# Softmax weights turned by VectorE in 32x32 blocks and by DMA, in place of TensorE transposes

## The reference, cut to what matters

```python
q, k, v, f, z = jnp.split(h @ w_in, SPLIT0, axis=-1)      # 12 query heads, 4 key/value heads, head width 128
q, k = apply_rope(q, ...), apply_rope(k, ...)
# blocks of 128 queries; each sees its own block, the one before and the one after, and 256 context tokens
s_win = einsum('bqkgd,bjkd->bkgqj', qn, kw) * scale
s_ctx = einsum('bqkgd,bjkd->bkgqj', qn, k_ctx) * scale
logits = concatenate([sink_logits, s_ctx, s_win], -1)
p = softmax(logits, -1)                                    # the sink takes part in the sum only
out = p_ctx @ v_ctx + p_win @ vw
y = concatenate([out, fourier_mix(f, w_f)], -1)
x = x + gate * ((y * silu(z)) @ w_out)
```

## Time and profile before

| | us |
|---|---|
| median of 3 runs | 1417.44 (1417.28 to 1417.67) |
| profiled execution, span from first to last instruction | 1416.2 |
| PE busy in it | 1389.8 (98%) |
| DVE busy | 861.2 (61%) |
| ACT busy | 515.2 (36%) |
| POOL busy | 74.6 (5%) |

### The profile page before, as it was taken

One profiled execution on the slowest core, in us unless ns is written; L12 is line 12 of the kernel. 1 busy time (PEld: TensorE's weight loads), 2 busy tenths in 40 slices (PEclk: granted clock), 3 DMA queues, 4 the chain that ended last, 5 costly groups with the idle time before them and its releaser, 6 DMA issues.

```text
span 1416.2 us, 19552 instructions
## 1 busy us (share of the span) xinstructions
PE 1389.8 (98%) x7474; PEld 1166.9 (82%) x7474; DVE 861.2 (61%) x1359; ACT 515.2 (36%) x798; POOL 74.6 (5%) x144
## 2 busy tenths in 40 slices
PE   4999999999999999999999999999999999999998
PEld 2788888888888888888888888888888888887887
DVE  6545655656778676776546685677666334474434
ACT  5323422244556444454222342122363223323332
POOL 0001111011100000000100101000000000010000
PEclk9999999999999999999999999999999999999999
DMA  9996567656712121224766656356523333365323
GB/s 384 407 390 245 184 212 243 195 183 207 223 46 64 56 75 52 67 89 132 234 188 190 197 181 214 92 165 193 177 90 105 92 102 91 106 203 182 111 89 119
DMA packets 64169, 232.75 MB, mean 164 GB/s; under 512 B 7120, under 2 KB 8144, under 8 KB 62816
## 3 DMA queue, kind: packets, MB, share of 16 engines
q1 hardware_dynamic: 42624, 154.23, 32.8%
q0 software_dynamic: 19792, 72.39, 16.3%
q10 hardware_dynamic: 1680, 5.10, 1.1%
HBM read 227.50 MB, written 4.19 MB: 164 GB/s over the span
## 4 chain that ended last, share of the span: by engine, by line
PE 92%; DVE 3%; DMA 2%; ACT 2%; SPq 1%; issue 1%; POOL 0%; POOLq 0%; DVEq 0%; ACTq 0%
PE ps L1439 90%; PE ps L1668 2%; DMA kvmem<-in_ctxT 1%; DMA modchunk<-in_modb 1%; DVE w_lo L857 1%; SPq L370 0%; ACT w_hi L452 0%; DVE modchunk L863 0%; ACT scratch L557 0%; DVE kvmem L1038 0%; PE ps L1793 0%; DVE pt_lo L1174 0%; ACT pt_hi L668 0%; ACT main L801 0%; DVE main L957 0%
## 5 line engine op out<-in xcount | busy, mean ns | idle before, releaser
L1439 PE MATMUL ps<-h_hi,w_hi 128*128 128x512 f32 x1592 | 625.8, 393 | 2.2 <-DVE w_lo L857 1.2
L1439 PE MATMUL ps<-h_hi,w_lo 128*128 128x512 f32 x1592 | 618.8, 389 | 0.0
L1439 PE MATMUL ps<-h_lo,w_hi 128*128 128x512 f32 x1592 | 618.4, 388 | 0.0
L857 DVE TENSOR_TENSOR w_lo<-raw,w_hi 128x1024 fp32r<-128x1024 f32 x206 | 252.3, 1225 | 372.3 <-ACT w_hi L452 372.0
L452 ACT CAST w_hi<-raw 128x1024 fp32r<-128x1024 f32 x206 | 216.1, 1049 | 600.2 <-PE ps L1439 599.9
L1439 PEld LDWEIGHTS ps<-h_hi,w_hi 128*128 128x128 f32 x1592 | 299.0, 188 | 65.7 <-issue 4.7
L1439 PEld LDWEIGHTS ps<-h_hi,w_lo 128*128 128x128 f32 x1592 | 298.9, 188 | 62.8
L1439 PEld LDWEIGHTS ps<-h_lo,w_hi 128*128 128x128 f32 x1592 | 299.2, 188 | 58.7
L863 DVE CUSTOM_DVE_ANT_0 modchunk<-modchunk,cond_row 128x1024 f32<-128x1024 f32 x128 | 154.6, 1220 | 22.2 <-DMA modchunk<-in_modb 22.0
L408 POOL DMA_DIRECT2D modchunk<-in_modb x128 | 67.9, 530 | 1114.9 <-DVE modacc L863 1090.9
L668 ACT CAST pt_hi<-ps 128x512 fp32r<-128x512 f32 (+1 forms) x48 | 30.7, 640 | 110.7 <-PE ps L1668 110.7
(11 more groups left out here) (232 smaller groups left out, 1364.5 us busy)
## 6 DMA issues: line engine op xcount, KB each, us to landing
raw<-in_weights SPq DMA_DIRECT2D x208, 512.0 KB, 3.6
modchunk<-in_modb POOLq DMA_DIRECT2D x128, 512.0 KB, 4.7
raw<-in_mod SPq DMA_DIRECT2D x32, 512.0 KB, 9.0
modchunk<-in_mod SPq DMA_DIRECT2D x16, 512.0 KB, 7.4
cond_row<-in_mod SPq DMA_DIRECT2D x16, 512.0 KB, 8.8
main<-in_xT SPq DMA_DIRECT2D x4, 1024.0 KB, 8.3
main<-in_xT ACTq DMA_DIRECT2D x4, 1024.0 KB, 5.0
out<-pooled SPq DMA_DIRECT2D x16, 256.0 KB, 2.8
```

Source lines behind the costliest of these rows:

```text
L857: nc.vector.tensor_tensor(low, src, high.bitcast(F32), ALU.subtract).then_inc(lo_ready, 1)
L1439: return nc.tensor.matmul(out, lhsT, rhs, start=start, stop=stop, skip_group_check=True)
```

## The change

The weights of a step are no longer scaled before they are turned, and PE no longer turns them.

1. DVE turns each 32x32 block of the exponents in place of the scaling (`turn_blocks`, 128x512 or 128x640 into `blocks_out`, which lies in `cond_row`). SP stores them to DRAM (`store_blocks`, 256 or 320 KB; 4 buffers there). POOL loads them back in four DMAs of 32 partitions, each fetching runs of 128 or 160 floats (512 or 640 bytes) from DRAM, so that the blocks land where a full transpose has them (`fetch_blocks`, two buffers `blocks_in`, in `cond_row` and `modchunk`). ACT and DVE then split them as before, from SBUF in place of PSUM (`turned_hi`, `turned_lo`), three slots after the exponents (`TURN_LAG`) and not one.
2. The row sums of three heads are inverted once a block (`invert_sums`), stored and loaded back as a row on every partition (`store_inverse`, `fetch_inverse`), and multiply the finished block (`block_out`, in place of the copy).
3. A head has 16 slots, two bank steps in nearly each; the attend slots are 6, 9, 12 and 15. The next head's keys are split in slot 12 and its first scores and maximum done in slot 14. Loops over heads are written out.
4. The rotation of the last four query tiles is spread over heads 0 and 1. The last head splits 8 tiles of y in its slots, and 4 right behind them.
5. POOL's modulation loads stop for the heads. Behind them `cond_row` is loaded again from a copy in DRAM (`row`), and the first set of jobs runs as (0, 1, 1, 1, 2, 1, 1, 1). Reloads of x: one in the last head, one behind it, two in `G_O`, in place of three and one.
6. The output product waits for the last block only at its fourth bank.

```diff
+LATER_JOBS = (0, 1, 1, 1, 2, 1, 1, 1)
-UNIT_SLOTS = (2, 4, 6, 7, 9, 10, 13)
-TILE_SLOTS = (2, 4, 6, 7, 9, 11)
-BANK_STEPS = (3, 2, 2, 2, 3, 2, 2, 3, 2, 2, 3, 2, 2, 2)
-BLOCK_SLOTS = (4, 7, 10, 13)
+SLOTS = 16
+UNIT_SLOTS = (2, 4, 6, 8, 10, 12, 13)
+PAIR_SLOTS = (4, 7, 10, 13)
+BANK_STEPS = (2,) * 11 + (3, 3, 2, 2, 0)
+BLOCK_SLOTS = (6, 9, 12, 15)
+TURN_LAG = 3
+NEXT_KEYS, NEXT_SCORES = 12, 14
+SWAP_SLOTS = (1, 7)
...
+            def store_blocks(i, k):
+                g, cols = i * STEPS + k, key_tiles(k) * P
+                sp.wait_ge(turned, g + 1)
+                sp.dma_start(turn_scratch[g % 4, :, 0:cols], blocks_out[g % 2][:, 0:cols]).then_inc(written[g % 2], 16)
...
+            for i in range(KV_HEADS):
+                for k in range(SLOTS):
+                    if 3 <= k <= STEPS and k % GQA == 0:
+                        fetch_inverse(i, k // GQA - 1)
+                    if k < STEPS and (k or i == 0):
+                        store_blocks(i, k)
+                    if k < STEPS and k % GQA == GQA - 1:
+                        store_inverse(i, k // GQA)
+                    if k == NEXT_SCORES and i + 1 < KV_HEADS:
+                        store_blocks(i + 1, 0)
+                    if k in UNIT_SLOTS:
+                        load_unit((G_Z + i) * HALVES + UNIT_SLOTS.index(k) + 6)
...
+            def fetch_blocks(i, k):
+                g, cols = i * STEPS + k, key_tiles(k) * P
+                run = cols // 4
+                pool.wait_ge(written[g % 2], 16 * (g // 2 + 1))
+                if g >= 2:
+                    pool.wait_ge(pt_ready, g - 1)
+                for j in range(4):
+                    pool.dma_start(blocks_in[g % 2][j * QUADRANT:(j + 1) * QUADRANT, 0:cols].rearrange("c (a x) -> c a x", a=4),
+                                 turn_scratch[g % 4, :, j * run:(j + 1) * run].rearrange("(a c) x -> c a x", a=4)
+                                 ).then_inc(pt_landed[g % 2], 16)
...
+            pool.dma_start(cond_row[:], row_scratch.broadcast_to([P, D])).then_inc(row_back, 16)
+            pool.wait_ge(y_done, KV_HEADS * BLOCKS)
+            load_chunks(M_O * HALVES // 2, M_END * HALVES // 2)
...
+            def turned_hi(i, k):
+                g = i * STEPS + k
+                act.wait_ge(pt_landed[g % 2], 64 * (g // 2 + 1))
+                if k % GQA == 0 and g:
+                    act.wait_ge(pv_done, g // GQA)
+                nc.scalar.copy(turned_tiles(k, pt_hi), landed_tiles(i, k)).then_inc(pt_hi_ready, 1)
...
-            def probabilities(i, k):
-                par = k % 2
-                dve.wait_ge(exp_done, i * STEPS + (k + 1))
-                chain.link(nc.vector.reciprocal(stat[:, 3, par:par + 1], stat[:, 2, par:par + 1]))
-                p = probs[par][:, 0:score_width(k) - 1]
-                nc.vector.tensor_scalar(p, p, stat[:, 3, par:par + 1], None, ALU.mult).then_inc(probs_ready, 1)
+            def turn_blocks(i, k):
+                g, cols = i * STEPS + k, key_tiles(k) * P
+                dve.wait_ge(exp_done, g + 1)
+                if g >= 2:
+                    dve.wait_ge(written[g % 2], 16 * (g // 2))
+                nc.vector.transpose(blocks_out[g % 2][:, 0:cols].rearrange("p (j t c) -> p j t c", j=4, c=QUADRANT),
+                                    probs[k % 2][:, 0:cols].rearrange("p (t j c) -> p j t c", j=4, c=QUADRANT)).then_inc(turned, 1)
...
-            def turn(i, k):
-                pe.wait_ge(probs_ready, i * STEPS + (k + 1))
-                if k and k % GQA == 0:
-                    pe.wait_ge(y_done, i * BLOCKS + k // GQA)
-                for t in range(score_width(k) // P):
-                    ins = nc.tensor.transpose(ps_flat[:, 6 * 512 + t * P:6 * 512 + (t + 1) * P],
-                                              probs[k % 2][:, t * P:(t + 1) * P], ident)
-                ins.then_inc(turned, 1)
```

313 lines of the change are left out of this document (197 added, 116 removed).

## The result

The changed kernel takes 1434.78 us (median of 4 runs, 1432.67 to 1437.16), the kernel before 1417.56 beside it (1417.28 to 1417.86): a ratio of 1.0123 with a 95% interval of 1.0110 to 1.0136, 17 us slower. Forecast was 1396 with a range to 1412. The rival that came true is the first, the round trip through DRAM, at a shorter trip than it had asked for.

A forecast was written before the change was run, and what follows sets the result against it. PE, saturated in the heads, was taken as the bound: -23.8 for transposes, -0.4 idle, +2.5 stalls, DMA nothing, so -21.7 from the 1416.2 us span gives 1394.5, said as 1396. Own range 1393 to 1400, whole range to 1412.

The forecast's parts named there:

- What PE loses: In the heads, 216 transposes leave PE: 23.8 us, a head falling from 69.15 to 63.2 us.
- What DVE gets: Each step swaps a reciprocal and a scaling for a block transpose of 0.84 or 0.71 us: 1.5 us more a head.
- rival 3: DVE becomes the bound in the heads if a block transpose costs 1.55 us: +8 us, 1404; chance 0.10.
- Near misses of DVE's turn: PE stalls by tenths where DVE lags, in some slots and behind the last head: sum 1.9, taken as 2.5 us.
- What DMA gets: The turned weights' trip through DRAM in the heads fits its three-slot cover and costs 0 us.
- L: Time from the end of a step's block transpose to its data back in SBUF: 6.9 to 8.4 us.
- rival 1: DMA round trip sets the head's time; slower than before beyond L = 13.0; 1442 us at L = 14.5; chance 0.12.
- free lag: How far DVE's maximum may fall behind in a slot before PE waits for it: 1.85 us.
- the rival's own formula: Least time of a head, four trips in a row plus two plain slots: 63.2 us at L = 11.5.
- The inverses: Their trip out and back in the heads has three slots, over 10 us, and so costs nothing.
- The rule on DMA transposes: Skill page's 19 times slower DMA transpose, some 5 ms more over 48 steps; thought not to apply; chance 0.02 inside rival 1.
- Rivals 1 and 2: The second is a milder late trip, L near 12.2 or two-buffer loop late: 1404 to 1412 us; chance 0.12 each.

The follow-up runs named there:

- own_blocks: Changed kernel without the stores and fetches of the turned exponents; ACT and DVE split what DVE wrote, so output is wrong; 1395.8 us, ratio 0.9849 to the kernel before.
- small_inverses: Changed kernel with the inverses fetched back to one partition instead of 128 (1.5 KB, not 192 KB), output scaled wrongly; 1427.9 us, ratio 1.0070 to the kernel before.

## Why the prediction was wrong, step by step

**What PE loses: right.** The page of own_blocks has PE at 1367.0 us, 22.8 less than before, where 23.8 was reckoned, and a middle head of it takes 63.9 us from its first turn to the next head's, against 63.2; the window nearest to it:

```profile
446.00:510.00 64.00, 63.60 (x320) 54.89 (x319) 51.63 (x87) 36.98 (x76) 0.00 (x0) 1.00 0.31 79
```

**What DVE gets: right.** The block transposes of the changed kernel (duration min/median/max) are the 0.84 and 0.71 us read off; rival 3's 1.55 is out. DVE's busy time as a whole grows by 2.5 us (861.2 to 863.7 in own_blocks), where 1.5 a head was put:

```profile
L1274 DVE STREAM_TRANSPOSE cond_row<-kvmem x9: 702/842/846, 401.6 to 495.5; 128x640 f32<-128x640 f32 x6, 128x512 f32<-128x512 f32 x3
```

**Near misses of DVE's turn: right in size.** 2.5 us were taken; PE is idle for 1.5 in the first 252 us of own_blocks' heads. With DMA at nothing these three parts came to a span of 1394.5 and a time of 1396; the kernel without the trip has 1394.0 and 1395.8. That it is so close is partly luck: PE lost 1.0 us less than reckoned and stood some 1.5 us less.

**What DMA gets: wrong, and this is the step that failed.** "So DMA costs nothing in my sum; its cover is the three-slot lag." Two terms of it were off.

The length. L was put at 6.9 to 8.4 us and is 11.2.

| term | taken | measured, mean |
|---|---|---|
| turn to store landed | 3.0 | 3.5 (2.0 alone, up to 9.1) |
| POOL's first issue to its fourth | 1.6 | 1.7 |
| start of the last issue to the last landing | 2.0 to 3.5 | 4.8 (2.1 alone, up to 7.4) |
| hand-overs, and waits for a free buffer | 0.3 | 1.2 |

Each price was read from a transfer that had the engines nearly to itself: the 2.0 us of the earlier trace rows is a 64 KB load, and the last fetch of step 0 of a head, alone too, takes 2.1. "The heads start from a DMA share of 0.20" was the argument against rival 1. But the share is a mean, and the bandwidth was there (108 GB/s were added, fewer than the 140 reckoned): 512 KB unit loads, a store and two steps' fetches fall into the same few us. The earlier trace rows held the warning, 9.0 us for 512 KB loads with many in flight, and the prediction quoted it for the rival only.

The room, and what is behind it. The prediction allowed 8.6 us plus 1.85 of free lag, and by the rival's own formula, 4(L + 2.5) + 7.3 for a head, nothing is lost up to L = 11.5. By that formula L = 11.3 gives a head of 62.5 us; it took 72.8. DVE's turns in head 1 show the terms (start, us, ...):

```profile
461.98 0.71 DVE L1274 STREAM_TRANSPOSE cond_row<-tmp 128x512 f32<-128x512 f32 x1 [0.89 <-ACT tmp L743]
...
475.58 0.84 DVE L1274 STREAM_TRANSPOSE cond_row<-kvmem 128x640 f32<-128x640 f32 x1
...
490.02 0.85 DVE L1274 STREAM_TRANSPOSE cond_row<-tmp 128x640 f32<-128x640 f32 x1 [0.25 <-ACT tmp L743]
495.53 0.84 DVE L1274 STREAM_TRANSPOSE cond_row<-kvmem 128x640 f32<-128x640 f32 x1
...
511.21 0.71 DVE L1274 STREAM_TRANSPOSE cond_row<-tmp 128x512 f32<-128x512 f32 x1
526.70 0.70 DVE L1274 STREAM_TRANSPOSE cond_row<-kvmem 128x512 f32<-128x512 f32 x1
534.74 0.71 DVE L1274 STREAM_TRANSPOSE cond_row<-tmp 128x512 f32<-128x512 f32 x1 [0.88 <-ACT tmp L743]
```

These are steps 1, 4, 7, 8, 11, and steps 0 and 1 of the next head. Where a step is turned behind the split of the step three before it, the two are a link. The same distances in own_blocks, where no trip is waited for, give what is PE's own pace (its steps 4 and 7 are shown):

```profile
463.42 0.85 DVE L1266 STREAM_TRANSPOSE cond_row<-kvmem 128x640 f32<-128x640 f32 x1 [0.39 <-ACT kvmem L735]
...
477.84 0.84 DVE L1266 STREAM_TRANSPOSE cond_row<-tmp 128x640 f32<-128x640 f32 x1 [0.25 <-ACT tmp L735]
```

| from turn to turn, head 1 | L of the first | changed kernel | own_blocks |
|---|---|---|---|
| step 1 to 4 | 11.4 | 13.6 | 10.4 |
| 4 to 7 | 10.7 | 14.4 | 14.4 |
| 7 to 8 | | 5.5 | 3.7 |
| 8 to 11 | 11.8 | 15.7 | 13.7 |
| 11 to 0 of the next head | 11.5 | 15.5 | 12.7 |
| 0 to 1 | | 8.0 | 8.8 |
| head | | 72.8 | 63.9 |

Two things in the formula were off. The two pieces outside the links take 12.5 us even in own_blocks, where two plain slots of 7.3 were put: the formula's loop began at step 0, whose trip is short, and the loop that binds begins at step 1. And a link takes 2.2 to 4.0 us over its L, 3.5 on the mean and not 2.5: DVE's low part, the query pieces and units lie between as well. Nor do all links bind: from 4 to 7 the trip costs nothing, the 9 us of this head are lost in the other three links and between 7 and 8. The mean hides that each link takes its own L: steps 1, 3, 7 and 11 mostly take 11 to 14 us (in head 1 a whole unit load moves beside the fetch of each; every fetch but that of step 0 has part of one beside it), and what one link loses the next doesn't give back.

So rival 1 was right in kind. It had said that the kernel gets slower only beyond L = 13.0; it did so at a mean of 11.2. The failed step is thus the cover: it set 6.9 to 8.4 us against 8.6 of room and 1.85 of lag, and the trip takes 11.2, more than both together.

**The inverses: nearly right.** That they have "three slots, over 10 us" was true, and neither DVE nor PE waited for them. But small_inverses is 7 us faster: 192 KB read from one row land among the blocks. The reload of `cond_row` and the stretch behind the heads are in own_blocks too, and cost nothing there, as said.

**The rule on DMA transposes.** In the changed kernel a step's blocks land in 4.1 us where nothing else moves, so the 19 times of the Trainium skill ("VectorE: DVE Perf Modes", The three transpose paths) is not what happened. The page itself ties its warning to a large innermost stride at the destination, which these runs of 512 and 640 bytes don't have. The loss came from an ordinary trip's latency under load.

The chances were 0.81 for faster. Rivals 1 and 2 together had 0.24, and the argument that kept them there was a mean share.

## What to carry to other kernels

Price a DMA on a dependent path from the landings of transfers that had as much company as it will have, and give every hop its own term: store, hand-over, issues, the slowest of the pieces. Then write down each loop of the schedule with its real instructions in between, check the loop's own pace, take the slowest step of it and not the mean, and ask what stands behind the waiting instruction on its engine: here a late landing on ACT held back the units, which have nothing to do with it. When room is lacking, room made by reordering a full slot was paid for in that slot; sending fewer steps on the trip, here with a slot more for each, bought it for less.
